# Pool columns projected in groups of 512 tokens with stationary weights, in the input stage of a fused transformer layer

## What is computed

```python
h = rms_norm(x, norm1_g)
proj = einsum('bsd,de->bse', h, w_in)           # [u | q | k | v], 1280 columns
# pool mixer: 4 groups of 128 channels, trailing windows 2, 4, 8, 16
pooled[g] = window_sum(u[g], w) / min(t + 1, w) - u[g]
a = einsum('bsgc,gcd->bsgd', pooled, pool_w) * pool_scale
# chunked sliding-window attention, q and k normalised per head, ALiBi, sinks
b = softmax_with_sink(q k^T / 8 - slope * dist) v
x = x + concat(a, b) @ w_out
x = x + square(relu(rms_norm(x, norm2_g) @ w_up)) @ w_down
```

## Time and profile before

| | us |
|---|---|
| runs of the kernel | 873.96, 873.99, 1765.8 |
| median | 873.99 |
| the profiled execution | 873.97 |
| its span, first to last instruction | 871.4 |

### The profile page before, as it was taken

How to read it: one execution, slowest core, us unless ns; L and a number is a source line. 1 busy time by engine, 2 the same in 40 slices (tenths; PEclk the granted TensorE clock), 3 DMA queues, 4 the chain that set the end, 5 groups by cost and what they waited for, 6 DMA issues and landing times.

```text
span 871.4 us, 10973 instructions
## 1 busy us (share of the span) xinstructions
PE 864.4 (99%) x4134; PEld 716.2 (82%) x4134; DVE 529.6 (61%) x802; ACT 418.4 (48%) x746; POOL 267.7 (31%) x202
## 2 busy tenths in 40 slices
PE   8999999999999999999999999999999999999998
PEld 6888888788888888888888888888888888888887
DVE  7666558944458666666666656467745464646463
ACT  7466658632236655555555555444333333333330
POOL 0633444300231342222333222004444004444440
PEclk9999999999999999999999999999999999999999
DMA  8311232552111565444555442889742453242422
GB/s 350 122 49 49 92 103 49 170 180 86 49 48 33 192 192 165 133 134 133 168 179 157 161 133 85 301 326 388 260 173 97 169 193 120 93 149 94 148 94 76
DMA packets 66485, 128.38 MB, mean 147 GB/s; under 512 B 3585, under 2 KB 20225, under 8 KB 66433
## 3 DMA queue, kind: packets, MB, share of 16 engines
q1 hardware_dynamic: 66144, 127.55, 42.8%
q10 hardware_dynamic: 288, 0.14, 0.1%
HBM read 89.92 MB, written 37.75 MB: 147 GB/s over the span
## 4 chain that ended last, share of the span: by engine, by line
PE 89%; DVE 5%; DMA 2%; ACT 2%; POOL 1%; issue 1%; SPq 0%; ACTq 0%; DVEq 0%; POOLq 0%
PE bank L1266 28%; PE bank L1268 28%; PE bank L1267 28%; DMA mem<-in_w_in 2%; PE bank L1381 1%; DVE ring L1038 1%; PE bank L1279 1%; PE bank L1366 1%; PE bank L1396 1%; POOL mem L507 1%; DMA raw<-in_w_up 1%; PE bank L1356 1%; DVE wgt L937 1%; DVE h_set L1070 1%; DVE t_M L1046 1%
## 5 line engine op out<-in xcount | busy, mean ns | idle before, releaser
L1266 PE MATMUL bank<-b_op,s_op 128*128 128x512 f32 (+1 forms) x450 | 174.8, 388 | 0.0
L1268 PE MATMUL bank<-b_op,s_op 128*128 128x512 f32 (+1 forms) x450 | 174.7, 388 | 0.0
L1267 PE MATMUL bank<-b_op,s_op 128*128 128x512 f32 (+1 forms) x450 | 174.7, 388 | 0.0
L575 POOL TENSOR_TENSOR b_sum<-d_raw,d_raw 128x1024 f32<-128x1024 f32 x40 | 95.9, 2398 | 202.2 <-DVE b_op L1081 202.2
L1077 DVE TENSOR_TENSOR s_op<-s_in,s_op 128x1024 fp32r<-128x1024 f32 x56 | 76.6, 1369 | 127.2 <-ACT s_op L778 127.2
L778 ACT ACTIVATE s_op<-s_in 128x1024 fp32r<-128x1024 f32 x56 | 59.4, 1060 | 177.6 <-PE bank L1268 147.8
L1266 PE MATMUL bank<-wgt,xs 128*128 128x256 f32 (+1 forms) x320 | 121.0, 378 | 1.3 <-DVE wgt L931 1.1
L1267 PE MATMUL bank<-wgt,xs 128*128 128x256 f32 (+1 forms) x320 | 118.3, 370 | 0.0
L1268 PE MATMUL bank<-wgt,xs 128*128 128x256 f32 (+1 forms) x320 | 118.2, 369 | 0.0
L1038 DVE TENSOR_TENSOR ring<-raw,ring 128x512 fp32r<-128x512 f32 x96 | 88.3, 933 | 31.0 <-ACT ring L726 29.5
L1266 PE MATMUL bank<-xs,ring 128*128 128x512 f32 x256 | 99.8, 390 | 0.1
(11 more groups left out here) (131 smaller groups left out, 1354.7 us busy)
## 6 DMA issues: line engine op xcount, KB each, us to landing
s_in<-h_keep SPq DMA_DIRECT2D x56, 512.0 KB, 3.7
h_keep<-h_set SPq DMA_DIRECT2D x16, 1280.0 KB, 5.1
raw<-in_w_up SPq DMA_DIRECT2D x16, 1024.0 KB, 6.4
d_raw<-in_w_down SPq DMA_DIRECT2D x32, 512.0 KB, 7.2
mem<-in_x SPq DMA_DIRECT2D x16, 512.0 KB, 5.9
h_keep<-h_set SPq DMA_DIRECT2D x16, 512.0 KB, 3.8
mem<-in_w_in SPq DMA_DIRECT2D x8, 640.0 KB, 8.0
mem<-in_x_T SPq DMA_DIRECT2D x8, 512.0 KB, 3.6
```

The source lines that it names most:

```text
L575: nc.gpsimd.tensor_tensor(out=b_sum[G % 2], in0=group_rows(qa, g), in1=group_rows(qb, g), op=op).then_inc(b_summed, 1)
L1266: nc.tensor.matmul(out_ap, lhs[HI], rhs[HI], start=first, stop=False, skip_group_check=chained)
L1267: nc.tensor.matmul(out_ap, lhs[HI], rhs[LO], start=False, stop=False, skip_group_check=chained)
L1268: return nc.tensor.matmul(out_ap, lhs[LO], rhs[HI], start=False, stop=last, skip_group_check=chained)
```

## The change

- u leaves the per-tile projection. `project_qkv(t, ks)` does 256 + 512 columns a k-step with the token tile stationary. `project_u(h, g, ks)` does one group of 128 channels for half the sequence, 512 tokens, with the weights stationary and the tokens moving. Its result is already transposed, so `copy_u`, the u transposes and `evac_u` go.
- The inverse rms now has to lie along the free dimension. SP writes each tile's column of 128 values to memory (`turn_rinv`, eight DMAs) and reads a half back as a row broadcast to all partitions (`load_rinv_row`, two). `scale_u` on DVE multiplies by it.
- Window sums, pooling and mixing go by half and group (8 times) and not by tile. A group of window 2^(g+1) gets g+1 adds, 20 in all, over 528 columns. `mix(h, g)` is three fp32r matmuls of 512 columns; so pooled values and `pool_w` are split (`pooled_high`, `pooled_low`, `split_map`). `mix_high` and `mix_low` are one instruction of 512 columns each.
- Tile 1 gets banks 5 and 6 for its projection, so it doesn't wait for the copies of tile 0. `score(0)` then waits for tile 1's copies.
- `w_in` is loaded and split in two parts: eight row blocks of 768 columns first, in eight buffers, then the u columns in four loads of two row blocks. `w_out` now passes through three staging buffers in place of five.
- `softmax_tail` makes one multiply with a broadcast operand per head group in place of four.
- The order on every engine is written out anew; transposes, probabilities and scores stand between other k-steps than before.

```diff
+            def load_w_qkv(k):
+                sp.dma_start(w_qkv_stage[k], w_in_k[k][:, POOL_W:IN_W]).then_inc(w_qkv_in[k], 16)
+            def load_w_u(j):
+                sp.dma_start(w_u_stage[j], w_u_pair[j][:, :, 0:POOL_W]).then_inc(w_u_in[j], 16)
+            def turn_rinv(t):
+                sp.wait_ge(rinv_ready, t + 1)
+                sp.dma_start(rinv_keep[t // KH, t % KH].rearrange("(p i) -> p i", i=1), rinv[:, t:t + 1]).then_inc(rinv_kept, 16)
+            def load_rinv_row(h):
+                sp.wait_ge(rinv_kept, 16 * KH * (h + 1))
...
             load_xT(0)
-            for k in range(6):
-                load_w_in(k)
+            for k in range(KT):
+                load_w_qkv(k)
             load_x(0)
...
+            load_w_u(0)
+            load_w_u(1)
+            load_xT(2)
+            load_w_u(2)
+            load_w_u(3)
+            load_x(1)
+            load_x(2)
+            turn_rinv(0)
+            turn_rinv(1)
+            load_xT(3)
+            load_x(3)
+            load_xT(4)
+            turn_rinv(2)
+            load_x(4)
+            turn_rinv(3)
...
+            load_rinv_row(0)
...
-        w_out_stage = [view(a, D) for a in (a_ws, a_ws + D, a_x, a_x + D, a_xn)]
-        W_OUT_SLOT = [0, 1, 2, 3, 4, 0, 1, 4]
+        w_out_stage = [view(a, D) for a in (a_x, a_xn, a_x + D)]
+        W_OUT_SLOT = [0, 1, 2, 0, 1, 2, 0, 1]
...
             def split_w_out(k):
-                sc.wait_ge(in_done, KT * (NT - 1) + (2 * D * (k + 1) - 1) // (2 * IN_W) + 1)
+                if k < KT // 2:
+                    sc.wait_ge(u_done, 2 * GROUPS)
...
+            def pooled_high(h, g):
...
+                nc.scalar.activation(pooled_part(h, g)[:, HI, :], u_T[:, g, HALO:UB], ACT.Copy).then_inc(pooled_hi, 1)
...
+            def scale_u(h, g):
...
+                nc.vector.tensor_tensor(out=u_T[:, g, HALO:UB], in0=bank[U_B[g % 2]][:, :], in1=rinv_row,
+                                        op=ALU.mult).then_inc(u_ready, 1)
...
+                    scale = inv_den[s].rearrange("p (h a) -> p h a", a=1).to_broadcast([P, PAIRS, P])
+                    nc.vector.tensor_tensor(out=scores[s], in0=scores[s], in1=scale, op=ALU.mult).then_inc(probs_ready, 1)
...
+            def project_u(h, g, ks):
...
+                    last = passes(bank[U_B[g % 2]][:, :], [w_u_s[:, k, part, cols] for part in (HI, LO)],
+                                  [xs[k // KH, h][:, part, k % KH, :] for part in (HI, LO)], k == 0, k == KT - 1)
...
+            def mix(h, g):
+                n = GROUPS * h + g
+                cols = slice(g * P, (g + 1) * P)
+                pe.wait_ge(pooled_lo, n + 1)
...
+                last = passes(bank[U_B[g % 2]][:, :], [pool_map[:, part, cols] for part in (HI, LO)],
+                              [pooled_part(h, g)[:, part, :] for part in (HI, LO)], True, True)
```

The new order on PE in its first and last parts, and what stands on ACT ahead of the second score and ahead of tile 5's scores:

```diff
+            project_qkv(0, range(KT))
+            project_qkv(1, range(KT))
+            transpose_in(0)
+            project_qkv(2, range(KH))
+            score(0)
+            project_qkv(2, range(KH, KT))
+            transpose_in(1)
+            project_u(0, 0, range(KT))
+            project_u(0, 1, range(5))
+            transpose_probs(0)
+            project_u(0, 1, range(5, KT))
+            score(1)
...
+            project_qkv(6, range(5, KT))
+            score(5)
+            project_qkv(7, range(1))
+            attend(4)
+            project_qkv(7, range(1, 6))
+            transpose_in(6)
+            project_qkv(7, range(6, KT))
+            mix(1, 0)
+            mix(1, 1)
+            transpose_probs(5)
+            project_out(0, range(0, 1))
+            score(6)
...
+            for k in range(4, 8):
+                split_w_u(k)
+            sum_squares_x(2)
+            sum_squares_x(3)
+            exponentials(0)
+            x_high(4)
+            evac_qk(1)
+            copy_kv(2)
+            copy_q(2)
+            sum_squares_x(4)
+            evac_probs(0)
...
+            for k in range(0, 4):
+                split_w_out(k)
+            evac_qk(5)
+            evac_probs(4)
+            copy_kv(6)
+            copy_q(6)
```

More of the change, by code:

```diff
@@ L589, in sum_squares @@
                     sc.wait_ge(sumsq_ready, T)
[L590 removed]
+                out = src if T < NT else junk
+                nc.scalar.activation(out, src, ACT.Square, accum_out=ssq[:, T:T + 1]).then_inc(sumsq_ready, 1)
             def sum_squares_x(t):
@@ new lines, in _ @@
+            softmax_head(0)
+            softmax_tail(0)
+            x_low(4)
+            place_values(2)
+            head_sums(2)
+            x_low(5)
+            head_norm(2)
+            scale_u(0, 0)
+            split_map()
+            pooled(0, 0)
+            scale_u(0, 1)
+            softmax_head(1)
+            softmax_tail(1)
+            pooled(0, 1)
+            x_low(6)
+            place_values(3)
+            head_sums(3)
+            x_low(7)
+            head_norm(3)
+            scale_u(0, 2)
@@ new lines, in _ @@
+            softmax_tail(3)
+            mix_low(0, 2)
+            mix_low(0, 3)
+            place_values(5)
+            head_sums(5)
+            head_norm(5)
+            scale_u(1, 0)
+            scale_u(1, 1)
+            softmax_head(4)
+            attention_low(3)
+            softmax_tail(4)
+            pooled(1, 0)
+            scale_u(1, 2)
+            pooled_low(1, 0)
+            pooled(1, 1)
+            scale_u(1, 3)
+            split_w_out(0)
+            pooled(1, 2)
+            split_w_out(1)
```

767 lines of the change are left out of this document (459 added, 308 removed).

## The result

The changed kernel takes 887.99 us (median of 6 runs, 887.24 to 889.13), the kernel before 873.96 (6 runs): a ratio of 1.0162, 95% interval 1.0152 to 1.0172. The forecast was 869.2 with a range of 865.5 to 873.5. It missed by 18.8 us and in sign. From the first product of `up` to the end the profile has 614.5 us, and 614.2 before, so the difference lies ahead of `up`, as was forecast.

A forecast was written before the change was run, and what follows sets the result against it. PE's instruction list was taken as the bound. PE work -7.0, waits that go -1.8, start +0.7, new waits +3.0, changes of form +0.3 gave -4.8 us from 873.97: 869.2 us, range 865.5 to 873.5.

The forecast's parts named there:

- Costed at nothing: Extra DVE instructions, ACT's changed work and the inverse-rms turn through memory: hidden under PE's list, 0 us.
- place 2: score(1) waits for evac_probs(0), since SP issues x loads behind sums of squares and inverse-rms turns: 1.2 us (0 to 3).
- The list of TensorE, -7.0: PE's work: u transposes -3.5, old mix -7.9, new mix +5.4, projection -1.0 us.
- E: Rival: the change takes no work from PE, for instance the wide mix as dear as the old; 873.2 us, chance 0.04.
- The start, +0.7: Smaller first weights start PE at 6.9 us, gain 0.7; tile 0 paced by DVE's splits, cost 1.4.
- place 1: transpose_in(0): normalised heads of tile 0 ready at 25.4, PE there at 24.9; 0.5 us (0 to 1.5).
- Place 3: score(5) late because w_out row block 3 waits for a staging buffer until DVE splits block 0; 0.6 us (0 to 3).
- D: Rival: slower than before, w_out block 3 lands late and ACT and PE stand for it; 875 us, chance 0.06.
- Place 4: transpose_probs(5) late behind DVE's head norm, two softmax heads and two low parts; 0.5 us (0 to 1.5).
- place 5: project_out(2) waits for both halves of the first add_x1; 0.2 us (0 to 1).
- Rival C: DVE and POOL block each other at 122 to 134 us, ahead of place_values(6): +3 us, 872.2 us, chance 0.17.
- rival B: The five forecast waits don't come: 866.2 us, or 865.0 with a smooth start; chance 0.25.

The follow-up runs named there:

- pe_turn: Changed kernel with the inverse-rms row turned on TensorE by four transposes and one copy a half, no DMA; 874.85 us, ratio 1.0008 to the kernel before.
- wide_order: pe_turn with VectorE and GpSimd work reordered, and the row through memory in one write of 16-byte packets a half; 870.93 us, ratio 0.9968.
- before_turns: Kernel before with only the eight inverse-rms writes added on SP, read by nothing; 881.51 us, ratio 1.0084.
- four_fixes: pe_turn with four small multiplies, later pooled(0, 2), attention_low(4) ahead of softmax_head(5), first two transpose_in one k-step later; 876.04 us, ratio 1.0024.
- slot_turn: Changed kernel with the eight 4-byte-packet writes 16 bytes apart, row read from norm2_g; 876.31 us, ratio 1.0025.
- sums_later: pe_turn with pooled(0, 2) behind softmax_tail(2) on VectorE, so GpSimd's additions start later; 873.18 us, ratio 0.9997.

## Why the prediction was wrong, point by point

**The step that failed.** "Costed at nothing" has the inverse-rms turn: 4.1 us to land after the row of the columns, nothing on the path. It asked only when the row is there for VectorE. The row was indeed late, for the write of tile 3 was issued at 48.41 and landed 12.88 us later, but VectorE waited only 1.33 us for it. The cost came by SP. The forecast counted the turns' waits for GpSimd (place 2), and never what eight writes under way do to the loads issued behind them, nor that SP stands until the write has landed before it issues the next load (11.6 us). And the price it took was that of a read into SBUF, in rows of 72 bytes for each partition, for a write of single words side by side. Put at nothing, it measured 13.2 us.

**The list of TensorE, -7.0: right in kind, 3 us too large.** The mix in pe_turn, start to start, first and last of two groups and the k-step behind them:

```profile
78.55 0.40 PE L1476 MATMUL bank<-pooled_even,pool_map 128*128 128x512 f32 x1
...
79.94 0.28 PE L1476 MATMUL bank<-wgt,xs 128*128 128x256 f32 x1
...
80.99 0.28 PE L1476 MATMUL bank<-wgt,xs 128*128 128x256 f32 x1
```

Six matmuls in 1.39 us, 0.232 each and not 0.227. With the wider gaps around some of them all 24 take 5.7 us in pe_turn and 6.2 in wide_order, for 5.4. A k-step of q, k and v takes 1.05 us, as forecast (0.34 + 0.70 = 1.04). The u columns run at 0.227 once under way (in the changed kernel from 120.06 to 122.56, 11 matmuls), but each stream starts with one of 0.32 behind transposes or scores, and over all 192 the timeline gives 0.2325. So the projection gained next to nothing of its 1.0, and the 0.3 us for changes of form was too small. Over the whole list the table below gives -3.9 for -7.0. That E is wrong and the list did shrink, wide_order shows: it beats the kernel before with more waits than that has.

**The start, +0.7.** The first product starts at 6.69 us, forecast 6.9 (before 7.56; 6.90 in pe_turn), and `transpose_in(0)` at 25.74, forecast 25.4.

**The five waits, 3.0 us.** In the changed kernel place 1 (`transpose_in(0)`) cost 0.75 for 0.5. Place 2 (`score(1)` for `evac_probs(0)`) cost 1.47 for 1.2, but by the late loads: in pe_turn it isn't there. Place 3 (block 3 of w_out) never came. In pe_turn ScalarE stood 3.40 us for the block at 135.8, yet it had landed some 3 us after its issue at 132.54, and `score(5)` started without a wait; D, which needs 9.6 us, falls with it. Place 4 cost 0.18 for 0.5, place 5 nothing. In their stead stood two that weren't on the list, the second half of the probabilities of tile 2 (2.15) and the key transpose of tile 6 (1.15). With place 1 (0.82 in pe_turn) and 0.4 at `transpose_in(1)` that is 4.5 of pe_turn's 5.8 us; the rest are five waits of under 0.4 each.

**Rival C had the mechanism and the wrong place.** It took GpSimd and VectorE blocking each other at 122 to 134 us, for 3 us. In pe_turn the splits and additions ahead of `place_values(6)` run from 124.7 to 142.6. The four additions of `window_sums(1, 3)` took 6.41 us, 1.6 each (over the 1.5 named as C's sign), and behind them came the 1.15 us at tile 6. But the dearer meeting was at 81 to 86 us, 2.15 us and the lower clock behind it, about 1.5.

**The sum.** The timeline of TensorE gives it, distances from start to start; "waits" are the idle times that it shows, "list" is the rest:

| us | before | changed | pe_turn | wide_order |
|---|---|---|---|---|
| first product starts | 7.56 | 6.69 | 6.90 | 6.95 |
| list up to `up` | 248.1 | 248.4 | 246.3 | 244.2 |
| waits up to `up` | 1.5 | 17.7 | 5.5 | 4.1 |
| first product of `up` | 257.19 | 272.78 | 258.70 | 255.25 |
| from there to the end | 614.2 | 614.5 | 614.3 | 614.5 |

wide_order has no turn on TensorE and no stretch at the lower clock, so its list shows the change alone: 3.9 us shorter, where -7.0 was forecast. The u transposes gave 3.4 (3.5 forecast), the mix 1.8 (2.5), the probabilities' transposes 0.4; the products of projection and `project_out` together take 1.6 us more, where -1.0 and +0.3 were put. In that 1.6 are the 0.17 us that hide beside each wait and the wide first gap of each stream. pe_turn's list has 0.8 us of turns and about 1.6 of lower clock on top, the changed kernel's about 4 us, an estimate from 248.4 - 244.2, of two stretches at the lower clock. So the changed kernel's 15.9 us of span are waits +16.2, clock +4, list -3.9, start -0.9, and 0.3 behind. For the waits +3.0 and -1.8 were forecast. The forecast's own sign, PE's waits "above 6 us", pointed at the right view. A slip in rival B: with its own terms a smooth start gives 864.8, not 865.0.

**What stays open.** The sum was made against 873.97, which is the span of 871.4 and 2.6 us around it. In all changed kernels there are 1.8 us or so around the span, and in before_turns 2.4. This 0.7 us speaks for the change and nothing here explains it. With no waits wide_order would take 870.9 - 4.1 = 866.8 us, an estimate near B's 866.2. It wasn't reached; that VectorE is the bound for 50 us before that is argued from waits that come back, and no run shortens VectorE's list to show it.

## What to carry to other kernels

A DMA is not costed by its bytes and its landing alone: ask what stands behind it on its queue, and where its packets fall. And ask what waits for the landing: where the issuing engine does, every load behind it waits too. Eight turns of a column of 128 numbers into part of a row, by single words side by side, cost 7.6 us in all when nobody read them and 13.2 where SP waited for them; gather four columns into one write, give the words room, or turn the column on TensorE. When work is taken from the bound engine, count the second engine's list, with its waits for the third, over the same stretch: here a wait taken from TensorE came back at the next place where it needed VectorE, and became smaller when work was moved into VectorE's own idle time.

## What the runs showed of the hardware

- Eight writes to memory of 128 packets of 4 bytes: median landing 7.9 us (up to 12.9) side by side, 9.2 in the kernel before, 3.0 with 16 bytes from one to the next, 2.8 with 64. Two writes of 16-byte packets side by side took 3.1. While the slow ones are under way the DMA engines are 45% busy at 56 GB/s, and 512 KB loads behind them take up to 11.2 us.
- TensorE's granted clock fell to the lower level (0.50 in a window of 2 us) during or after waits of 5.59 us (changed kernel), 4.74 (before_turns) and 2.80 (four_fixes), and after waits of 2.15 us with only transposes run shortly before (pe_turn, changed kernel); wide matmuls then came 0.43 us apart. It did not always fall: the same wait of 2.15 us in slot_turn, behind one of 0.92, and one of 2.21 at 89.23 in the changed kernel left it at 1.00. A kernel whose longest wait in its trace was 1.95 us (sums_later) had 1.000 in six executions and 0.998 in four.
- VectorE's multiplies of 128x128 with one operand in SBUF took 2.34 us for four beside GpSimd's additions, 0.88 without. Instructions of 128x4 that take 0.16 or 0.17 us took 0.95 to 1.23 beside them.
- A multiply of 128x512 with its SBUF operand read at a stride of 16 bytes took 1.06 us, 0.69 without the stride.
